# Attention values turned round for two heads at once, with the probabilities scaled on ScalarE before they are transposed

## The reference, cut to what matters

```
p_c = masked_softmax(q @ kc.T * scale + bias)      # over 31 compressed keys
p_s = masked_softmax(q @ ks.T * scale + bias)      # "slc"
p_w = masked_softmax(q @ kw.T * scale + bias)      # "win"
o = g0 * (p_c @ vc) + g1 * (p_s @ vs) + g2 * (p_w @ vw)     # g: sigmoid gates, one per token, head and branch
y = concat([o, conv]) @ w_out
```

## Time and profile before

| | us |
|---|---|
| median of 3 runs | 1429.01 |
| lowest, highest | 1426.13, 1436.88 |
| span of the profiled execution | 1428.9 |
| PE busy in it | 1371.8 |
| attention stage, slot 0 to the last value matmul | 843.7 to 1004.6 |

### The profile page before, as it was taken

How to read it: one execution, slowest core, us unless ns; L and a number is a source line. 1 busy time by engine, 2 the same in 40 slices (tenths; PEclk the granted TensorE clock), 3 DMA queues, 4 the chain that set the end, 5 groups by cost and what they waited for, 6 DMA issues and landing times.

```text
span 1428.9 us, 23064 instructions
## 1 busy us (share of the span) xinstructions
PE 1371.8 (96%) x9570; PEld 1131.4 (79%) x9570; DVE 698.6 (49%) x1192; ACT 566.9 (40%) x854; POOL 465.6 (33%) x131
## 2 busy tenths in 40 slices
PE   5999999999999999999999999999999999999998
PEld 3788766776788888888888678888798888888886
DVE  6656686464665333353337435687255454453002
ACT  4435654253342223222125445555364433443112
POOL 0243143024314434434522321121212443344344
PEclk9999999998999999999999999999999999999999
DMA  8763266002222232223214420011222223223311
GB/s 333 249 138 118 71 244 220 3 4 84 94 89 89 92 115 89 89 102 134 89 62 164 167 89 31 30 38 53 75 89 89 89 89 114 93 89 109 112 59 59
DMA packets 24741, 147.93 MB, mean 104 GB/s; under 512 B 2716, under 2 KB 3868, under 8 KB 9024
## 3 DMA queue, kind: packets, MB, share of 16 engines
q1 hardware_dynamic: 21128, 134.21, 26.6%
q10 hardware_dynamic: 3512, 12.26, 3.2%
HBM read 141.74 MB, written 4.72 MB: 103 GB/s over the span
## 4 chain that ended last, share of the span: by engine, by line
PE 87%; DVE 7%; ACT 2%; issue 2%; DMA 1%; POOL 1%; SPq 0%; DVEq 0%; ACTq 0%; POOLq 0%
PE bank L2090 24%; PE bank L2092 23%; PE bank L2091 23%; PE bank L2397 5%; PE bank L1168 2%; DMA raw<-in_weights 1%; PE bank L1159 1%; PE bank L1150 1%; DVE xres L1692 1%; PE bank L2276 1%; DVE act_lo L1689 1%; POOL xres L1330 1%; PE bank L2257 1%; DVE bank L1685 1%; PE bank L1077 1%
## 5 line engine op out<-in xcount | busy, mean ns | idle before, releaser
L1301 POOL TENSOR_TENSOR weight_lo<-raw,weight_hi 128x2048 fp32r<-128x2048 f32 (+2 forms) x90 | 415.1, 4612 | 822.9 <-ACT weight_hi L1349 822.8
L2090 PE MATMUL bank<-act_hi,weight_hi 128*128 128x512 f32 (+1 forms) x1136 | 433.1, 381 | 6.0 <-DVE q L879 1.9
L2092 PE MATMUL bank<-act_hi,weight_lo 128*128 128x512 f32 (+1 forms) x1136 | 422.8, 372 | 0.0
L2091 PE MATMUL bank<-act_lo,weight_hi 128*128 128x512 f32 (+1 forms) x1136 | 422.6, 372 | 0.0
L1349 ACT ACTIVATE weight_hi<-raw 128x2048 fp32r<-128x2048 f32 (+1 forms) x98 | 185.2, 1890 | 393.4 <-PE bank L2092 392.3
L2090 PEld LDWEIGHTS bank<-act_hi,weight_hi 128*128 128x128 f32 x1136 | 214.0, 188 | 48.0 <-issue 8.3
L2092 PEld LDWEIGHTS bank<-act_hi,weight_lo 128*128 128x128 f32 x1136 | 213.7, 188 | 38.6
L2091 PEld LDWEIGHTS bank<-act_lo,weight_hi 128*128 128x128 f32 x1136 | 214.1, 188 | 34.7 <-issue 0.5
L2090 PE MATMUL bank<-weight_hi,hid_hi 128*128 128x512 f32 x352 | 136.9, 389 | 0.0
L2091 PE MATMUL bank<-weight_lo,hid_hi 128*128 128x512 f32 x352 | 136.9, 389 | 0.0
L2092 PE MATMUL bank<-weight_hi,hid_lo 128*128 128x512 f32 x352 | 136.9, 389 | 0.0
(11 more groups left out here) (376 smaller groups left out, 1755.3 us busy)
## 6 DMA issues: line engine op xcount, KB each, us to landing
raw<-in_weights SPq DMA_DIRECT2D x120, 1024.0 KB, 4.8
w<-in_w ACTq DMA_DIRECT2D x2, 2048.0 KB, 12.0
bias_rows<-grow ACTq DMA_DIRECT2D x1, 2560.0 KB
xres<-in_x SPq DMA_DIRECT2D x4, 512.0 KB, 5.8
strip<-bias_rows ACTq DMA_DIRECT2D x1, 2048.0 KB, 9.8
out<-xres SPq DMA_DIRECT2D x3, 512.0 KB, 2.6
row_a<-in_ln_g ACTq DMA_DIRECT2D x2, 512.0 KB, 4.1
row_b<-in_ln_b ACTq DMA_DIRECT2D x2, 512.0 KB, 4.9
```

The source lines that it names most:

```text
L1301: pool.tensor_tensor(wlo[i % SPLIT][:, :size], raw[n % RAW][:, :size], whi[i % SPLIT][:, :size], ALU.subtract).then_inc(lo_ready, 1)
L2090: pe.matmul(o, l[0], r[0], start=first, stop=False)
L2091: pe.matmul(o, l[0], r[1], start=False, stop=False)
L2092: return pe.matmul(o, l[1], r[0], start=False, stop=last)
```

## The change

Items are ordered by pairs of heads: for each pair and tile, slc of both heads, then win of both. ACT multiplies the probabilities in place by gate over sum (new semaphore `probs_scaled`), one item behind the exponential; `turn2` of slc and win items waits for that. The value product is done once for two heads: the values (128x64) are stationary, the turned probabilities (128 tokens) move, and the two heads write to the two column halves of bank 4, so that the result comes out with features by row. Both branches and the compressed branch of a pair accumulate in that bank over all four tiles; ACT and DVE split it into `out_hi` and `out_lo` once for each pair. DVE's addition to `o`, ACT's copy of the cmp values, and `turn_o` with its splits are gone. The turned probabilities have four buffers for two, and the shared banks of the stage are three (5 to 7).

```
@@ -369,9 +369,13 @@
-ITEMS = [item for h in range(N_HEADS) for i in range(TT)
-         for item in ([("cmp", None, i)] if h == 0 else []) + [("slc", h, i), ("win", h, i)]]
+ITEMS = [item for k in range(PAIRS) for i in range(TT)
+         for item in ([("cmp", None, i)] if k == 0 else []) + [(br, 2 * k + c, i) for br in ("slc", "win") for c in range(2)]]
 CMP_AT = [ITEMS.index(("cmp", None, i)) for i in range(TT)]
+HEAD_ITEMS = [n for n, item in enumerate(ITEMS) if item[0] != "cmp"]
+PROBS_AT = {n: at for at, n in enumerate(HEAD_ITEMS)}
+PAIR_END = [ITEMS.index(("win", 2 * k + 1, TT - 1)) for k in range(PAIRS)]
+TURNED = 4
 N_SLOTS = len(ITEMS) + 3
 SLOT_UNITS = ("cg0", "cg1", "xt0", "xt1", "bg0", "bg1")
...
@@ -388,10 +392,15 @@
     return range(PER_UNIT * n, min(PER_UNIT * (n + 1), N_SLOTS))
+def second_of_pair(item):
+
+    return ITEMS[item][0] != "cmp" and ITEMS[item][1] % 2 == 1
+
+
 def stages_of(slot):
     return [(st, slot - lag) for st, lag in (("scores", 0), ("turn2", 2), ("values", 3))
-            if 0 <= slot - lag < len(ITEMS)]
+            if 0 <= slot - lag < len(ITEMS) and (st != "values" or second_of_pair(slot - lag))]
...
@@ -414,14 +423,16 @@
             b.add(("raw_hidden", "k" if name == "gates" else "v"), act=1)
     for name in ("win", "gates"):
         b.add(("turn_v", name), act=1)
+    b.shared = range(5, 8)
     for n, name in enumerate(SLOT_UNITS):
         dense(name, drains=[dict(act=1) if name[:2] == "cg" else dict(dve=1)] * 2)
         for slot in slots_of(n):
             for st, item in stages_of(slot):
-                by_act = st == "turn2" or (st == "values" and ITEMS[item][0] == "cmp")
-                b.add((st, item), **(dict(act=1) if by_act else dict(dve=1)))
-    for k in range(PAIRS):
-        b.add(("turn_o", k), act=1, dve=1)
+                if st == "values":
+                    b.add((st, item), 4, **(dict(act=1, dve=1) if item in PAIR_END else {}))
+                else:
+                    b.add((st, item), **(dict(act=1) if st == "turn2" else dict(dve=1)))
+    b.shared = range(4, 8)
     dense_rows("mix2", "out2_3", act=1)
     turned_halves("h4", dve=2, act=2)
...
@@ -562,8 +573,12 @@
     gate = here("gate", [P, TT, 24])
     bgT = here("bgT", [P, 4, SEQ])
     cgT = here("cgT", [P, 4, SEQ])
+    strip_at = nxt
     strip = here("strip", [P, N_HEADS, SEQ])
-    o = here("o", [P, TT, MIX])
+    out_parts, _ = place("attention_out", [P, N_HEADS, SEQ], F32R, strip_at)
+    out_hi, out_lo = (out_parts[:].rearrange("p (k a) n -> p a k n", a=2)[:, part] for part in range(2))
+    turned_probs = here("turned_probs", [P, 2, SEQ])
+    cmpT = here("turned_cmp", [P, TT, 2 * P])
...
     raw_hidden = acc[:, 3 * SEQ:3 * SEQ + CMP_HID]
-    probsT = [acc[:, 3 * SEQ:4 * SEQ], sc4[:]]
+    probsT = [acc[:, 3 * SEQ:4 * SEQ], sc4[:], turned_probs[:, 0, :], turned_probs[:, 1, :]]
     before_turn = {n: acc[:, SEQ * j:SEQ * j + SEQ] for j, n in enumerate(("slc", "win", "gates"))}
     row3, z = place("row3", [P, DM], F32, arena + 4 * TT * DM)
...
@@ -758,17 +773,21 @@
         a.done(act.activation(gate[:].rearrange("p t g -> p (t g)"), bank(("turn_v", "gates"))[:, 0:24 * TT], ACT.Copy),
                drain(("turn_v", "gates"), "act"))
-        for n, name in enumerate(SLOT_UNITS):
+        for n, unit in enumerate(SLOT_UNITS):
             convert()
             for slot in slots_of(n):
                 if 0 <= slot - 2 < len(ITEMS):
                     item = slot - 2
-                    w = n_keys(item) if ITEMS[item][0] != "cmp" else N_HEADS * CMP_W
                     await_full(act, ("turn2", item))
-                    if item >= 2:
-                        await_full(act, ("values", item - 2))
-                    b = bank(("turn2", item))
-                    a.done(act.activation(probsT[item % 2][:, 0:w], b[:, 0:w], ACT.Copy), drain(("turn2", item), "act"))
+                    if ITEMS[item][0] == "cmp":
+                        w, to = N_HEADS * CMP_W, cmpT[:, ITEMS[item][2], :]
+                    else:
+                        n, w = PROBS_AT[item], n_keys(item)
+                        to = probsT[n % TURNED][:, 0:w]
+                        if n >= TURNED:
+                            reader = HEAD_ITEMS[n - TURNED]
+                            await_full(act, ("values", reader if second_of_pair(reader) else reader + 1))
+                    a.done(act.activation(to, bank(("turn2", item))[:, 0:w], ACT.Copy), drain(("turn2", item), "act"))
                 if 0 <= slot < len(ITEMS):
...
@@ -777,25 +796,25 @@
                     else:
                         a.step(act.activation(scores[x][:, 0:w], scores[x][:, 0:w], ACT.Exp, bias=low[:, x:x + 1],
                                               scale=-1.0, accum_out=den[:, x:x + 1]), S["exp_done"])
-                if 0 <= slot - 3 < len(ITEMS) and ITEMS[slot - 3][0] == "cmp":
-                    i = ITEMS[slot - 3][2]
-                    await_full(act, ("values", slot - 3))
-                    a.done(act.activation(o[:, i, :].rearrange("p (g j d) -> p j g d", g=N_KV, d=HD),
-                                          bank(("values", slot - 3))[:].rearrange("p (j g d) -> p j g d", g=N_KV, d=HD), ACT.Copy),
-                           drain(("values", slot - 3), "act"))
-            if name[:2] == "cg":
+                if slot - 1 in PROBS_AT:
+                    item = slot - 1
+                    probs = scores[item % 3][:, 0:n_keys(item)]
+                    act.wait_ge(S["weight_ready"], PROBS_AT[item] + 1)
+                    a.done(act.activation(probs, probs, ACT.Copy, scale=weights4[:, item % 4:item % 4 + 1]), S["probs_scaled"])
+                if slot - 3 in PAIR_END:
+                    name = ("values", slot - 3)
+                    await_full(act, name)
+                    a.done(act.activation(out_hi[:, PAIR_END.index(slot - 3), :], bank(name)[:], ACT.Copy), drain(name, "act"))
+            if unit[:2] == "cg":
                 for j in range(2):
-                    await_full(act, (name, j))
-                    a.done(act.activation(cgT[:, 2 * int(name[2]) + j, :], bank((name, j))[:], ACT.Copy), drain((name, j), "act"))
+                    await_full(act, (unit, j))
+                    a.done(act.activation(cgT[:, 2 * int(unit[2]) + j, :], bank((unit, j))[:], ACT.Copy), drain((unit, j), "act"))
         act.wait_ge(S["upper_free"], 1)
         for k in range(4):
...
-            await_full(act, ("turn_o", k))
-            a.done(act.activation(act_hi[:, k, :], bank(("turn_o", k))[:], ACT.Copy), drain(("turn_o", k), "act"))
...
@@ -919,6 +938,12 @@
             else:
                 stt(bgT[:, k, tap:], cgT[:, k, 0:SEQ - tap], col("cmix", 8 - 4 * tap + k), bgT[:, k, tap:], ALU.mult, ALU.add)
+        def lo_of_pair(k):
+
+            name = ("values", PAIR_END[k])
+            await_drained(dve, name, "act")
+            tt(out_lo[:, k, :], bank(name)[:], out_hi[:, k, :].bitcast(F32), ALU.subtract, sem=drain(name, "dve"))
+
         def by_group(x):
...
@@ -969,15 +994,8 @@
                         cmp_scores(slot, i)
                     else:
                         head_scores(slot, h, i)
-                if 0 <= slot - 3 < len(ITEMS) and ITEMS[slot - 3][0] != "cmp":
-                    item = slot - 3
-                    br, h, i = ITEMS[item]
-                    oh = o[:, i, HD * h:HD * h + HD]
-                    await_full(dve, ("values", item))
-                    if h == 0:
-                        await_drained(dve, ("values", CMP_AT[i]), "act")
-                    stt(oh, bank(("values", item))[:, 0:HD], weights4[:, item % 4:item % 4 + 1], oh, ALU.mult, ALU.add,
-                        sem=drain(("values", item), "dve"))
+                if slot - 4 in PAIR_END:
+                    lo_of_pair(PAIR_END.index(slot - 4))
                 if 0 <= slot - 1 < len(ITEMS):
...
@@ -1004,10 +1022,7 @@
                     tt(bgT[:, k, :], bank((name, j))[:], bgT[:, k, :], ALU.mult, sem=drain((name, j), "dve"))
         for k in (2, 3):
             lo_of_convolution(k)
-        for k in range(PAIRS):
-            await_full(dve, ("turn_o", k))
-            await_drained(dve, ("turn_o", k), "act")
-            tt(act_lo[:, k, :], bank(("turn_o", k))[:], act_hi[:, k, :].bitcast(F32), ALU.subtract, sem=drain(("turn_o", k), "dve"))
+        lo_of_pair(PAIRS - 1)
...
@@ -1137,7 +1152,8 @@
                 br, h, i = ITEMS[item]
                 w = n_keys(item)
                 b = bank((st, item))
-                claim(pe, (st, item))
+                if st != "values" or (br, i) == ("slc", 0):
+                    claim(pe, (st, item))
                 if st == "scores" and br == "cmp":
                     for j in range(REP):
...
@@ -1154,20 +1170,24 @@
                     for m in range(2):
                         mm = pe.transpose(b[:, tok(m)], p8[:].rearrange("p h n -> p (h n)")[:, tok(m)], ident[:])
                 elif st == "turn2":
```

(47 more changed lines are left out.)

2 lines of the change are left out of this document (1 added, 1 removed).

## The result

The kernel after takes 1458.64 us (median of 4 runs, 1451.69 to 1460.72), the kernel before 1431.09 in the runs beside it: a ratio of 1.0188, with 95% between 1.0162 and 1.0215. The profiled execution spans 1458.9 us, 30.0 more than before. It is the slowest of the four: its granted clock over the whole program is 0.984, where the fastest (1451.69) has 0.991.

The account below looks back on a forecast made before the run. PE was taken to bound the kernel before. The stage was to grow from 160.9 to 179.6 us (+18.7), its end to gain 1.1: net +17.6, shaded to +16, so 1445 us, range 1422 to 1460.

Parts of the forecast that it names:

- The ring as summed: Attention-stage slots: copy, exponential, sum, scaling, transposes, copy again, none overlapping; 146.7 us for rings alone, 1438 to 1453, chance 0.50.
- the third rival, ring and clock: Ring holds and PE's idling lowers its clock in a third of the stage, some 15 us more: 1460, chance 0.12.
- One of the signs: Sign of being right: PE's transposes wait in most slots for ACT's scaling, 25 to 40 us in all.
- The ring's pieces: Hand-over, copy, exponential with sum, gap and scaling in a slot: 2.93, 2.52, 2.08, 1.64 us for 512 to 128 keys.
- a slot takes the longer of the two: Each attention slot lasts as long as its ring or PE's own work there, whichever is longer.
- PE's cases: Slots where PE's work, with values or more dense matmuls, exceeds the ring: 4 us added over the stage.
- the forecast's 5 us for convolution steps, late exponentials and splits: Stage extras: DVE's convolution steps, exponentials late after six dense matmuls, pair splits ahead of a weight; 5 us, between 0 and 10.
- 5.5 forecast with the drains: Five weight conversions on ACT between units, half exposed, 1.1 us each: 5.5; two drains after cg units listed separately, 2.2 together.
- The end of the stage: After the last values: output starts some 2.7 us behind, third product 6.35 against 7.47 now; a gain of 1.1 us.
- PE's saving: PE's work in the attention stage falls by 14.8 us, with new value matmuls at 0.055 us each.
- PE stays bound: Rival: the ring is hidden, the stage falls by 14.8 us and the end by 1.1: 1413 us, chance 0.10.
- shorter ring: Rival: hand-over through PE 0.15 us shorter in each of 64 slots, conversions hidden: 1428 to 1436, chance 0.28.

Follow-up runs that it names:

- e1: The changed kernel without ACT's scaling, transposes waiting for the exponential alone, the factor gate over sum left out: 1421.33 us, 0.9935 of before.

## Why the prediction was right, and where it was off

**Direction and mechanism.** The ring as summed was the likeliest case, and it is what happened: PE's waits for the scaling are 25.7 us (25 to 40 forecast), the same loss comes from the scaling alone, and the same instructions in another order, or one slot later, take it away again. The measured 1458.64 lies in the wide range (1422 to 1460), but 14 above the point and above the range given for the ring by itself (1438 to 1453). The nearest forecast is that of the third rival, ring and clock (1460), which had a chance of 0.12. So the mechanism was right, and the loss was put at 16 us where it is 28. One of the signs didn't come either: PE shows a wait for the scaling in 29 of the 64 slots, not in most.

**The ring's pieces.** Forecast 2.93, 2.52 and 2.08 us for 512, 384 and 256 keys, measured 2.86, 2.43 and 2.00. The hand-over for four transposes was 0.82 instead of 0.87. In slots where only the ring counts the forecast was thus 0.07 to 0.09 too high.

**The term that was mis-sized: the slots in which PE is the longer.** The step that failed is "a slot takes the longer of the two", with 4 us for PE's cases: it set PE's work and the ring of the same width side by side. What meets in a slot are the scores of item s, the transposes of s-2 and the values of s-3, and these differ in width. The first slot of 128 keys holds the values of the 512-key tile before, sixteen matmuls, and its transposes stand 911.04 - 908.81 = 2.23 us apart, where the ring has 1.64 and the forecast's worst case for PE 2.0.

```profile
908.81 0.30 PE L1175 MATMUL bank<-ident,acc 128*128 128x128 f32 x1 [0.72 <-ACT acc L803]
...
909.04 1.09 PE L1182 MATMUL bank<-turned_probs,vwn 128*64 128x128 f32 x16
...
911.04 0.29 PE L1175 MATMUL bank<-ident,acc 128*128 128x128 f32 x1
...
913.09 0.40 ACT L803 ACTIVATE acc<-acc,per_row 128x128 f32<-128x128 f32 x1 [0.74 <-DVE per_row L1699]
```

The run without the scaling (e1), where no ring can hold it, shows the same slot at the same 2.23 us, 896.35 to 898.58:

```profile
896.35 0.30 PE L1170 MATMUL bank<-ident,acc 128*128 128x128 f32 x1
896.58 1.09 PE L1177 MATMUL bank<-turned_probs,vwn 128*64 128x128 f32 x16
...
898.58 0.30 PE L1170 MATMUL bank<-ident,acc 128*128 128x128 f32 x1
```

Add up the forecast's own pieces for the widths that meet in each interval from transposes to transposes, and compare. In the last three pairs of heads, from 908.81 to 1032.75 us, thirteen of the 47 intervals are clearly longer than their ring though PE shows no wait; nine of them have the same length in e1 to 0.04 us. Together they are 7.6 us over the ring (the clock's part taken off), where PE's cases had 3 for these pairs.

**The other terms there.** The last row above is the pair's split, which stands on DVE ahead of the weight: with it the second slot of 128 keys took 2.60 us in each of the three pairs, 0.96 over its ring, 2.9 together; this was in the forecast's 5 us for convolution steps, late exponentials and splits, which came out at 5.1 in these pairs. The four intervals in which ACT is late by a conversion are 4.8 us over their ring, for 5.5 forecast with the drains.

**The clock.** A rival for itself in the prediction, with 15 us; it came beside the ring, with about 5. The granted clock was 0.50 (1.2 GHz) at the start of the stage and again from 900 us, behind waits of 1.16 and 1.37 us, and PE ran at the lower level a third time behind a wait of 1.75 us at 988 us, in windows of 0.84 and 0.82. It was back at 1.00 each time; with the filler the last two stretches stayed at 1.00. The Trainium skill's rule (TensorE: Matmul & The Clock Gate, "A second HAM failure mode") that brief, frequent idleness makes the clock go down and up agrees in kind; its share here was small. The error of the rival was to put a third of the stage at the low level.

**The sum.** The dense matmuls behind the stage came 30.6 us later where 18.7 was forecast, 11.9 more. In the last three pairs: PE's slots +4.6, clock +1.0, rings -1.5, conversions -0.7, the rest 0.1, together 3.6. Before 908.81 it is 8.0 more, of which the clock has 3.9; the other 4 are not told apart, since the first slots and three cmp slots lie there (the three intervals around the third cmp slot are 4.1 us over their rings, where 3.0 was forecast for it). Behind the last transposes 0.2. The end of the stage holds: the output starts 2.85 us behind the last values (2.7), the third product 6.44 behind (6.35), a gain of 1.03 (1.1). The shading by 1.6 us went the wrong way.

**PE's saving.** 14.8 us forecast; with the slot more the stage is 12.6 us shorter than before. By the rule of the Trainium skill that was weighed there (TensorE: Matmul & The Clock Gate, "The mechanism": a load overlaps only where the row group differs) the value matmuls would have taken 0.11 us each; measured are 0.0575, alternating, and even where the program doesn't alternate the halves came to overlap in part. The measurement decides: for this form the two column halves do run beside each other.

**The rivals.** *PE stays bound* would have been right with one slot more (1413 forecast, 1417.99 measured): its condition, that the ring is hidden, is what that edit makes. The *shorter ring* comes near the reordered kernel (1429.84), whose ring lacks the exponential. Of the two remedies the slot more is the better by 12 us.

## What to carry to other kernels

Where a step is added between two engines that each run in program order, don't ask whether the engine has room; write out the circle from one hand-over to the next, with all that stands in the program between them, and compare it with the bounding engine's work in the same slot, lags included. An engine that is busy in 62% of a stage (117.78 of 191.2 us) can hold the ring that bounds it. The remedy costs buffers, not instructions: the same work one slot later turned 1.9% slower into 0.9% faster.

## What the runs showed of the hardware

**DVE stands still beside GpSimd.** A DVE scaling from SBUF to SBUF (0.29 to 0.49 us) that was issued while GpSimd's 4.53 us subtraction ran ended 0.1 to 0.3 us behind it, after up to 4.36 us. The timeline of the kernel after has two such cases off the path: a convolution step that takes 0.75 us elsewhere took 2.79, below, and 2.45 at 979.89 us, while a step with an input from PSUM (L981) and one on a single column ran at their usual length.

```profile
947.53 4.55 POOL L1314 TENSOR_TENSOR weight_lo<-raw,weight_hi 128x2048 fp32r<-128x2048 f32 x1 [26.63 <-ACT weight_hi L1362]
...
948.86 0.29 DVE L981 CUSTOM_DVE_ANT_0 acc<-bank,strip 128x128 f32<-128x128 f32 x1 [1.59 <-PE bank L1166]
...
949.59 0.21 DVE L1699 TENSOR_SCALAR per_row<-per_row,gate 128x1 f32<-128x1 f32 x1
949.83 2.79 DVE L1705 SCALAR_TENSOR_TENSOR bgT<-cgT,params,bgT 128x511 f32<-128x511 f32 x1
```
The Trainium skill (SBUF — State Buffer, "SBUF: two separate sides") has this as an exclusive lock of the port pair that the two share, the later one blocking for the whole instruction, for a DVE operation in its two-port mode, or one with two SBUF inputs against a GpSimd operation that reads SBUF. The ends here agree with it, and the convolution step has two SBUF inputs; that the scaling runs in that mode no run shows by itself.

**Filling idle PE time gave as much as it took.** 29 us of matmuls whose result nobody reads left the time as it was (1457.0 against 1458.64). They kept the clock at 1.00 from 900 and 988 us on, where it had fallen, and brought the stage from 0.94 to 0.98, worth 4.9 us with the start; in the slots where PE had no idle time they cost about 0.5 us each.

**Two column halves overlap out of the program's order.** Fp32 matmuls with 64 stationary columns, first all of one half and then all of the other, took 1.73 us for twenty in one slot, where alternating ones took 1.24 and no overlap at all would take about 2.0 (20 x 0.10, an estimate from the first five, which ran alone). In the whole program the difference of the medians is 4.3 us, with intervals that overlap.
